# The weighed one-hot tile of the gate matrices: from a compare on VectorE and a multiply on ScalarE to one VectorE instruction per token

## The chip, the cores and the metric

The program runs on one core of one Trainium2 chip. The metric is the device time of one execution in microseconds (us). TensorE (PE) multiplies matrices into PSUM, VectorE (DVE), ScalarE (ACT) and GpSimd (POOL) work element by element on 128 partitions, and SyncE (SP) issues transfers. Each engine has a queue of its own and goes through it in order; engines wait for each other by semaphores.

## What is computed

One layer of a hybrid trunk for 576 frames (512 of a prompt, 64 of a running stream) of width 2048: two token mixers, then a retrieval of experts (PEER), then a norm. The change lies in the retrieval. Each token has 8 heads, each head picks 16 of 128 x 128 experts, and an expert's number is a pair of keys:

```python
idx = jnp.take_along_axis(cand_i, pos, axis=-1)          # i1 * 128 + i2
gate = jax.nn.softmax(best_s, axis=-1).astype(x.dtype)
...
hid = jax.nn.gelu(jnp.einsum('td,thkd->thk', xb, u_tab[ib]), approximate=False)
return jnp.einsum('thk,thkd->td', hid * gb, v_tab[ib])
```

For the first 384 tokens the kernel does not gather experts. It computes the hidden values of all 16384 experts and multiplies them by a gate matrix per token: 128 x 128 numbers, zero but for the up to 128 picks of the token. The other 192 tokens gather rows of the two tables.

## The kernel before

The matrix of one token is a product of two one-hot tiles over its 128 picks (8 heads x 16). Picks lie on the partitions. `i1T`, `i2T` and `gateT` (`idxT[0]` to `idxT[2]`, [128, 384]) hold, per pick and token, the first key, the second key and the gate. For a token, row p of the tile `oa` is zero but at key i1 of pick p, where the gate stands; row p of `ob` has a one at key i2. `ob` transposed times `oa` is the matrix.

Work goes in **units** of four tokens, 96 of them, in one stage of the program that is here called the gate stage:

- VectorE (`onehots`) compares the row `iota` (0 to 127) with four columns of `i1T` into `oa[u]` (128 x 512, four buffers, `NOH`), then the same for `i2T` into `ob[u]` (two buffers). Both are one TENSOR_TENSOR each, at L1669. An `oa` waits until TensorE has used that buffer four units ago, an `ob` until two units ago (`gmat_ps`).
- ScalarE (`weigh`, L1062) waits for `matched`, and multiplies each token's 128 x 128 part of `oa` in place by its column of `gateT`: four instructions per unit, one unit ahead. Then it copies the unit before out of PSUM (`gbuf`, L1074). After 12 units it also computes one GELU (L1081).
- TensorE (`gmats`, L2190) waits for `onehots` and `weighed`, and multiplies the unit's four tokens, 128 x 128 each, into one of four banks of `aux`.

TensorE has other work among these units: a **piece** is a weight block of 8 row blocks of 128, and each of its 8 steps is three matmuls of 128 x 384 (L1869). Six units stand in each piece, after steps 0, 2, 3, 5, 6 and 7 (`AFTER`), so the stage is 16 pieces. GpSimd prepares each piece once the one two before it is used: `wh` is a rounded copy of `wr` (L720), `wl` the rest (L722). SyncE loads the pieces, writes `gbuf` to memory after each 12 units and brings it back later as `gtile`. Before the gate stage VectorE picks the experts (top-k); behind it lie the value products with the streamed tables. All orders are written out by hand; there is no scheduler.

Of the kernel before, what the change touches and what calls it, by code (L numbers as in the profile page):

```python
# [17 lines left out]
ALU = mybir.AluOpType  # L18
ACT = mybir.ActivationFunctionType
# [6 lines left out]
TD = 384  # L26
# [12 lines left out]
NK = 128  # L39
# [4 lines left out]
TB = 48  # L44
NTB = TD // TB
# [14 lines left out]
NOH = 4  # L60
# [87 lines left out]
def trunk_program(nc, x_in, w_in, vec_in, const_in, s0_in, keys_in, u_in, v_in, y_out, sp_out, ss_out, dnc_out, scc_out,  # L148
# [49 lines left out]
    def const(name, rows=128):  # L198
        a, n = CONST[name]
        return cst[0:rows, a:a + n]  # L200

    def vector(name, j=None, n=1):
# [74 lines left out]
    oa = [r.take(f"oa{i}", [128, 4, NK]) for i in range(NOH)]  # L277
    ob = [r.take(f"ob{i}", [128, 4, NK]) for i in range(2)]
    gl = [sb(f"gl{i}", [128, TD], F32, gl_at + i * PC4) for i in range(2)]
    r = Region(rows_at, end)  # L280
    idxT = [r.take(n, [128, TD]) for n in ("i1T", "i2T", "gateT")]
# [56 lines left out]
        half_kept0 half_kept1 merged hb_in0 hb_in1 kept_z0 kept_z1 go_in0 go_in1 go_sq go_sum go_ss go_root go_step  # L338
        sig_kept0 sig_kept1 go_scaled go_hi go_lo
        mg_hi mg_lo xr_in0 xr_in1 keys_in score_ps topk_step scores_read shifted picked gate_exp pick_done pickT_ps  # L340
        pickT_done matched weighed onehots gmat_ps gmat_out gates_kept0 gates_kept1
        gt_in0 gt_in1 hid_kept0 hid_kept1 gl_in0 gl_in1 m_done m_hi m_lo tails_kept y_kept waited gelu_done alone_ready staged turned row_in0 row_in1 row_in2 row_in3 row_done raw_full2 hid_done coef_step sums_added""".split()
    S = {n: nc.alloc_semaphore(n) for n in names}

# [7 lines left out]
    def bank(slot, half):  # L352

        return ps[slot][:, half, 0:TD]
# [33 lines left out]
    def loop(eng, start, stop):  # L388

        return nc.Fori(start, stop, engines=bass.OrderedEngineSet([eng.engine]), hint_back_edge=True)  # L390

    def peel(eng, n, body):

        body(0)
        with loop(eng, 1, n) as i:
            body(i)
# [20 lines left out]
    UNITS = TB // 4  # L417
# [358 lines left out]
    def _(act):  # L776
# [76 lines left out]
        for g in range(2):  # L853
# [3 lines left out]
            last = act.activation(bar[:, 5:NCH, g, :],  # L857
                                  ps[0][:, 1, 5 * C - HT:HT].rearrange("p (n c) -> p n c", c=C), ACT.Copy)
# [24 lines left out]
        for v in range(H):  # L883
            m, u = 2 * H + v, v % 2
# [13 lines left out]
        for m in range(FIRST_Z, NZ):  # L898
            u = m % 2
# [155 lines left out]
                j += 1  # L1055

        def weigh(n, t0, u):

            act.wait_ge(S["matched"], n + 1)  # L1060
            for c in range(4):
                last = act.activation(oa[u][:, c, :], oa[u][:, c, :], ACT.Copy, scale=idxT[2][:, bass.ds(t0 + c, 1)])  # L1062
            last.then_inc(S["weighed"], 1)

        def gmats(i, final=False):
            for b in range(2):
                if not (isinstance(i, int) and i == 0):
                    act.wait_ge(S[f"gates_kept{b}"], 16 * i)
                for r_ in range(UNITS):
                    un = UNITS * b + r_  # L1070
                    if not (final and un == 2 * UNITS - 1):
                        weigh(2 * UNITS * i + un + 1, 2 * TB * i + 4 * un + 4, (un + 1) % NOH)
                    act.wait_ge(S["gmat_ps"], 2 * UNITS * i + un + 1)
                    act.activation(gbuf[b][:, :, 4 * r_:4 * r_ + 4],  # L1074
                                   aux[:, un % 4, :].rearrange("p (t i) -> p i t", t=4),
                                   ACT.Copy).then_inc(S["gmat_out"], 1)
                    hp = HPG + PLAIN + 2 * i + b
                    if r_ == UNITS - 1:
                        act.wait_ge(S[f"hid_kept{b}"], 16 * i + 16 * PLAIN // 2)
                        act.wait_ge(S["piece_used"], 2 * hp + 2)  # L1080
                        act.activation(gl[b][:, :], bank(b, 0), ACT.Gelu).then_inc(S[f"evacuated{b}"], 1)  # L1081

        weigh(0, 0, 0)
        gmats(0)
        with loop(act, 1, NTB // 2 - 1) as i:
            gmats(i)
        gmats(NTB // 2 - 1, True)

        def high(n, source):  # L1090
# [65 lines left out]
    def _(dve):  # L1156
        def wait(name, value):
            dve.wait_ge(S[name], value)
# [175 lines left out]
        for v in range(H):  # L1334
            u = v % 2
# [209 lines left out]
        for m in range(KD):  # L1545
            u = m % 2
# [117 lines left out]

        wait("pickT_done", 1)

        def alike(out, x, t0):

            return dve.tensor_tensor(out[:, :, :], const("iota").unsqueeze(1).to_broadcast([128, 4, NK]),  # L1669
                                     idxT[x][:, bass.ds(t0, 4)].unsqueeze(2).to_broadcast([128, 4, NK]),  # L1670
                                     ALU.is_equal)

        def onehots(i):
            for u in range(NOH):
                n = NOH * i + u
                if not isinstance(i, int):
                    wait("gmat_ps", n - NOH + 1)
                alike(oa[u], 0, 4 * n).then_inc(S["matched"], 1)
                if not (isinstance(i, int) and u < 2):
                    wait("gmat_ps", n - 1)  # L1680
                alike(ob[u % 2], 1, 4 * n).then_inc(S["onehots"], 1)

        peel(dve, TD // (4 * NOH), onehots)
        for u in range(2):
            wait(f"gates_kept{u}", 16 * NTB // 2)
# [10 lines left out]
        def kept_low(g, k):  # L1696

            n = G2 * g + k
            wait("m_hi", n + 1)
            dve.tensor_tensor(yp[:, n % (2 * G2), TD:2 * TD], gl[k % 2][:, :],  # L1700
                              yp[:, n % (2 * G2), 0:TD].bitcast(F32), ALU.subtract).then_inc(S["m_lo"], 1)
# [33 lines left out]
        def x_wide(b_):  # L1735

            if b_ == 0:
                dve.tensor_tensor(x_last[:, :, :], xa[:, :, TA - C:TA].bitcast(F32),
                                  xa[:, :, 2 * TA - C:2 * TA].bitcast(F32), ALU.add).then_inc(S["alone_ready"], 1)
                dve.tensor_tensor(held[:, :].rearrange("p (k t) -> p k t", t=128), xa[:, :, 0:128].bitcast(F32),  # L1740
                                  xa[:, :, TA:TA + 128].bitcast(F32), ALU.add).then_inc(S["staged"], 1)
            else:
                wait("alone_ready", 7)
                wait("turned", 2)
                dve.tensor_copy(held[:, :].rearrange("p (k c t) -> p k c t", c=2, t=C),
                                x_last[:, :, :].unsqueeze(2).to_broadcast([128, KD, 2, C])
                                ).then_inc(S["staged"], 1)
# [50 lines left out]
        kept_low(0, 0)  # L1798
        kept_gated(0, 1)
        kept_low(0, 1)  # L1800
        wait("weighed", TD // 4)
        x_wide(0)
        kept_gated(0, 2)
        kept_low(0, 2)
# [28 lines left out]
    def _(pe):  # L1833
# [27 lines left out]
        def piece(hp, c, slot, passes, k0, first, last, tiles_=range(NPIECE), done=("piece_used",),  # L1861
                  between=lambda t: None, ready=None):

            w = split_of(2 * hp + c) if isinstance(hp, int) and isinstance(c, int) else c % 2
            for t in tiles_:
                if ready:
                    ready(k0 + t)
                for weights, half, moving, more, final in passes(k0 + t - tiles_[0]):
                    mm_ = pe.matmul(ps[slot][:, half, 0:moving.shape[1]], weights[w][:, t, :], moving,  # L1869
                                    start=first and t == tiles_[0] and not more,  # L1870
                                    stop=last and t == tiles_[-1] and bool(final))
                if t < tiles_[-1]:
                    between(t)
            if done:
                mm_.then_inc(S[done[0]], 1)
# [302 lines left out]
        def gmats(i):  # L2178
            for b in range(2):
                hp = HPG + PLAIN + 2 * i + b  # L2180

                def unit(r_):
                    un = UNITS * b + r_
                    u = un % 4
                    pe.wait_ge(S["onehots"], 2 * UNITS * i + un + 1)
                    pe.wait_ge(S["weighed"], 2 * UNITS * i + un + 1)
                    if not (isinstance(i, int) and un < 4):
                        pe.wait_ge(S["gmat_out"], 2 * UNITS * i + un - 3)
                    for c in range(4):
                        last = pe.matmul(aux[:, u, c * NK:(c + 1) * NK], oa[un % NOH][:, c, :], ob[un % 2][:, c, :],  # L2190
                                         start=True, stop=True)
                    last.then_inc(S["gmat_ps"], 1)

                pe.wait_ge(S[f"evacuated{b}"], EV_G[b] + PLAIN // 2 + i)
                for c in range(2):
                    pe.wait_ge(S["lo_done"], 2 * hp + c + 1)
                    piece(hp, c, b, dense(xp, TD), NPIECE * c, c == 0, c == 1,
                          between=lambda t: unit(PER_PIECE * c + AFTER.index(t)) if t in AFTER else None)
                    unit(PER_PIECE * c + PER_PIECE - 1)
# [186 lines left out]
```

## Time and profile before

| | us |
|---|---|
| median of 3 runs | 4428.61 (4421.59 to 4431.16) |
| profiled execution, its own time | 4437.7 |
| its span in the trace | 4435.9 |
| PE busy | 4280.7 (97%) |
| DVE busy | 2552.9 (58%) |
| ACT busy | 1100.8 (25%) |
| POOL busy | 2657.0 (60%) |
| gate stage, first to last unit on TensorE | 2238.4 to 2422.5 |

The span is the time from the first to the last instruction in the trace. Busy shares are means over stages with different limits, so they don't say what the gate stage waits for. A duration in the trace reaches from an instruction's start to its end; successive instructions of one engine can overlap by a little, so from one start to the next it can be less than a duration.

### The profile page before, as it was taken

To read this page: it belongs to the slowest core of one execution; us is meant where nothing else is said; L and a number is where in the kernel's file an instruction comes from. 1 tells how busy PE (TensorE), PEld (TensorE's weight loads), DVE (VectorE), ACT (ScalarE), POOL (GpSimd) and SP (SyncE) were. 2 spreads that over 40 slices of the span, in tenths; PEclk is the share of its full clock that TensorE was granted. 3 is DMA by queue.
4 is the path that set the end of the run, shared out by engine and by line. 5 is a ranking of instruction groups with operands and counts; after the bars stand their busy time and mean duration, and the time that the engine had idled before them with its cause. 6 is when DMAs were issued, how large, how long until landed. Compare 5 with 4: busy or idle time off the path is not lost.

```text
span 4435.9 us, 73784 instructions
## 1 busy us (share of the span) xinstructions
PE 4280.7 (97%) x29840; PEld 4208.9 (95%) x29840; DVE 2552.9 (58%) x3551; ACT 1100.8 (25%) x1850; POOL 2657.0 (60%) x1516
## 2 busy tenths in 40 slices
PE   6999999999999999899999888999999999999997
PEld 6999999999999999899888888999999999999997
DVE  6863433322234421699577577777777776677744
ACT  4541000011011100100077122332322332323323
POOL 3555444444445555455743656888787787787863
PEclk9999999999999999999999999999999999999998
DMA  3333222222333443222446677999999998999963
GB/s 112 98 104 107 74 77 76 88 93 88 100 122 120 142 137 102 77 91 86 129 159 201 226 279 286 394 386 387 368 390 389 389 385 332 387 385 367 391 250 119
DMA packets 271697, 941.53 MB, mean 212 GB/s; under 512 B 59984, under 2 KB 101200, under 8 KB 221264
## 3 DMA queue, kind: packets, MB, share of 16 engines
q1 hardware_dynamic: 216144, 535.08, 35.1%
q0 software_dynamic: 55296, 402.68, 22.7%
q8 instruction: 203, 3.33, 0.3%
q14 instruction: 54, 0.44, 0.0%
HBM read 879.12 MB, written 58.55 MB: 211 GB/s over the span
## 4 chain that ended last, share of the span: by engine, by line
PE 80%; DVE 10%; DMA 4%; issue 2%; POOL 2%; ACT 1%; DVEq 0%; SPq 0%; ACTq 0%; POOLq 0%
PE ps L1869 74%; DMA wr<-in_w 3%; PE aux L2024 3%; POOL wl L771 2%; PE aux L2190 1%; DVE ob L1669 1%; DMA gl<-hid_s 1%; PE ps L1901 1%; DVE ti L1591 0%; DVE mrall L1592 0%; DVE ti L1599 0%; DVE cand L1601 0%; DVE sel L1630 0%; ACT wh L1112 0%; DVE sel L1635 0%
## 5 line engine op out<-in xcount | busy, mean ns | idle before, releaser
L771 POOL TENSOR_TENSOR wl<-wr,wh 128x1024 fp32r<-128x1024 f32 x444 | 1066.9, 2403 | 422.8 <-ACT wh L1112 421.5
L1869 PE MATMUL ps<-xp,wh 128*128 128x384 f32 x4544 | 1173.9, 339 | 9.8 <-POOL wl L722 6.8
L1869 PE MATMUL ps<-yp,wh 128*128 128x384 f32 x4096 | 1061.9, 340 | 37.0 <-POOL wl L771 15.0
L720 POOL CAST wh<-wr 128x1024 fp32r<-128x1024 f32 x338 | 369.0, 1092 | 1214.5 <-PE ps L1869 666.5
L1869 PE MATMUL ps<-xh,wh 128*128 128x288 f32 x3296 | 991.4, 301 | 1.6 <-DVE yt L1489 1.6
L1869 PE MATMUL ps<-xl,wh 128*128 128x288 f32 x3296 | 972.5, 295 | 0.0
L1869 PE MATMUL ps<-xh,wl 128*128 128x288 f32 x3296 | 969.1, 294 | 0.0
L722 POOL TENSOR_TENSOR wl<-wr,wh 128x1024 fp32r<-128x1024 f32 x338 | 839.6, 2484 | 27.1
L1869 PEld LDWEIGHTS ps<-xp,wh 128*128 128x128 f32 x4544 | 805.2, 189 | 12.1 <-issue 10.3
L1869 PEld LDWEIGHTS ps<-yp,wh 128*128 128x128 f32 x4096 | 750.7, 190 | 42.1 <-POOL wl L771 17.2
L1869 PE MATMUL ps<-xp,wl 128*128 128x384 f32 x2272 | 762.8, 336 | 0.0
L1112 ACT ACTIVATE wh<-wr 128x1024 fp32r<-128x1024 f32 x444 | 470.5, 1060 | 1043.4 <-PE ps L1869 680.0
L1869 PE MATMUL ps<-yp,wl 128*128 128x384 f32 x2048 | 696.0, 340 | 0.0
L1869 PEld LDWEIGHTS ps<-xh,wh 128*128 128x128 f32 x3296 | 617.6, 187 | 14.4 <-issue 5.4
L1869 PEld LDWEIGHTS ps<-xh,wl 128*128 128x128 f32 x3296 | 620.6, 188 | 0.0
L1869 PEld LDWEIGHTS ps<-xl,wh 128*128 128x128 f32 x3296 | 619.0, 188 | 1.0
L1766 DVE SCALAR_TENSOR_TENSOR aux<-rows,hid,aux 128x2048 f32<-128x2048 f32 x192 | 451.0, 2349 | 0.4
L1755 DVE SCALAR_TENSOR_TENSOR rows<-rows,aux 128x2048 f32<-128x2048 f32 x192 | 436.8, 2279 | 0.7 <-PE aux L2222 0.7
L1869 PEld LDWEIGHTS ps<-xp,wl 128*128 128x128 f32 x2272 | 428.3, 189 | 0.0
L1722 DVE TENSOR_TENSOR mg<-mg,ps 128x384 f32<-128x384 f32 x512 | 280.8, 551 | 253.1 <-PE ps L1869 252.8
L1869 PEld LDWEIGHTS ps<-yp,wl 128*128 128x128 f32 x2048 | 387.8, 189 | 0.0
L1709 DVE TENSOR_TENSOR ps<-ps,gtile 128x384 f32<-128x384 f32 x96 | 54.4, 567 | 322.0 <-ACT ps L1141 322.0
(295 smaller groups left out, 4382.6 us busy)
## 6 DMA issues: line engine op xcount, KB each, us to landing
wr<-in_w SPq DMA_DIRECT2D x786, 512.0 KB, 4.3
gates_s<-gbuf SPq DMA_DIRECT2D x8, 3072.0 KB, 11.8
gtile<-gates_s SPq DMA_DIRECT2D x32, 768.0 KB, 10.5
qkv<-qkv_s SPq DMA_DIRECT2D x9, 768.0 KB, 4.5
gl<-hid_s SPq DMA_DIRECT2D x32, 192.0 KB, 6.6
hid_s<-gl SPq DMA_DIRECT2D x28, 192.0 KB, 3.9
mg<-in_x SPq DMA_DIRECT2D x4, 1152.0 KB, 12.4
qkv_s<-lo SPq DMA_DIRECT2D x16, 288.0 KB, 3.0
```

What stands on the lines that cost most here:

```text
L720: pool.tensor_copy(high[u][:, :, :], wr[u][:, :, :]).then_inc(S["hi_done"], 1)
L722: pool.tensor_tensor(low[u][:, :, :], wr[u][:, :, :], high[u][:, :, :].bitcast(F32), ALU.subtract).then_inc(S["lo_done"], 1)
L771: pool.tensor_tensor(wl[q][:, :, :], wr[r_][:, :, :], wh[q][:, :, :].bitcast(F32), ALU.subtract).then_inc(S["lo_done"], 1)
L1112: act.activation(wh[q][:, :, :], wr[r_][:, :, :], ACT.Copy).then_inc(S["hi_done"], 1)
L1669: return dve.tensor_tensor(out[:, :, :], const("iota").unsqueeze(1).to_broadcast([128, 4, NK]), idxT[x][:, bass.ds(t0, 4)].unsqueeze(2).to ...
L1709: dve.tensor_tensor(own, own, gtile[g % 2][:, :, k, :], ALU.mult).then_inc(S["m_done"], 1)
L1722: dve.tensor_tensor(mg[:, j, 0:TD], mg[:, j, 0:TD], bank(x, d % 2), ALU.add).then_inc(S[f"evacuated{x}"], 1)
L1755: dve.scalar_tensor_tensor(rows[r_][:, :], rows[r_][:, :], 1.0, wide_aux, ALU.mult, ALU.mult, accum_out=hid[b_][:, j:j + 1]).then_inc(S["r ...
L1766: dve.scalar_tensor_tensor(wide_aux, rows[r_][:, :], hid[b_][:, j:j + 1], wide_aux, ALU.mult, ALU.add).then_inc(S["row_done"], 1)
L1869: mm_ = pe.matmul(ps[slot][:, half, 0:moving.shape[1]], weights[w][:, t, :], moving, start=first and t == tiles_[0] and not more, stop=las ...
L1901: mm_ = pe.matmul(ps[x][:, half, 0:moving.shape[1]], held[:, t, :], moving, start=k == 0 and not more, stop=k == KD - 1 and bool(final))
L2024: last = pe.matmul(out(h), left(h), right(h), start=start, stop=stop)
```

## The change

VectorE writes the weighed `oa` itself: per token one TENSOR_SCALAR that compares `iota` with the token's column of `i1T` and multiplies the result by its column of `gateT`, both given as one value per partition. ScalarE's `weigh` and the semaphores `matched` and `weighed` are gone. The order of the two tiles on VectorE, the buffers and the other waits stay.

```diff
@@ -1055,21 +1055,12 @@
                 j += 1
 
 
-        def weigh(n, t0, u):
-
-            act.wait_ge(S["matched"], n + 1)
-            for c in range(4):
-                last = act.activation(oa[u][:, c, :], oa[u][:, c, :], ACT.Copy, scale=idxT[2][:, bass.ds(t0 + c, 1)])
-            last.then_inc(S["weighed"], 1)
-
-        def gmats(i, final=False):
+        def gmats(i):
             for b in range(2):
                 if not (isinstance(i, int) and i == 0):
                     act.wait_ge(S[f"gates_kept{b}"], 16 * i)
                 for r_ in range(UNITS):
                     un = UNITS * b + r_
-                    if not (final and un == 2 * UNITS - 1):
-                        weigh(2 * UNITS * i + un + 1, 2 * TB * i + 4 * un + 4, (un + 1) % NOH)
                     act.wait_ge(S["gmat_ps"], 2 * UNITS * i + un + 1)
                     act.activation(gbuf[b][:, :, 4 * r_:4 * r_ + 4],
                                    aux[:, un % 4, :].rearrange("p (t i) -> p i t", t=4),
@@ -1080,11 +1071,7 @@
                         act.wait_ge(S["piece_used"], 2 * hp + 2)
                         act.activation(gl[b][:, :], bank(b, 0), ACT.Gelu).then_inc(S[f"evacuated{b}"], 1)
 
-        weigh(0, 0, 0)
-        gmats(0)
-        with loop(act, 1, NTB // 2 - 1) as i:
-            gmats(i)
-        gmats(NTB // 2 - 1, True)
+        peel(act, NTB // 2, gmats)
 
 
         def high(n, source):
@@ -1664,21 +1651,28 @@
 
         wait("pickT_done", 1)
 
-        def alike(out, x, t0):
+        def chosen(out, t0):
 
             return dve.tensor_tensor(out[:, :, :], const("iota").unsqueeze(1).to_broadcast([128, 4, NK]),
-                                     idxT[x][:, bass.ds(t0, 4)].unsqueeze(2).to_broadcast([128, 4, NK]),
+                                     idxT[1][:, bass.ds(t0, 4)].unsqueeze(2).to_broadcast([128, 4, NK]),
                                      ALU.is_equal)
+
+        def chosen_weighed(out, t0):
+
+            for c in range(4):
+                last = dve.tensor_scalar(out[:, c, :], const("iota"), idxT[0][:, bass.ds(t0 + c, 1)],
+                                         idxT[2][:, bass.ds(t0 + c, 1)], ALU.is_equal, ALU.mult)
+            return last
 
         def onehots(i):
             for u in range(NOH):
                 n = NOH * i + u
                 if not isinstance(i, int):
                     wait("gmat_ps", n - NOH + 1)
-                alike(oa[u], 0, 4 * n).then_inc(S["matched"], 1)
+                chosen_weighed(oa[u], 4 * n)
                 if not (isinstance(i, int) and u < 2):
                     wait("gmat_ps", n - 1)
-                alike(ob[u % 2], 1, 4 * n).then_inc(S["onehots"], 1)
+                chosen(ob[u % 2], 4 * n).then_inc(S["onehots"], 1)
 
         peel(dve, TD // (4 * NOH), onehots)
         for u in range(2):
@@ -1798,7 +1792,7 @@
         kept_low(0, 0)
         kept_gated(0, 1)
         kept_low(0, 1)
-        wait("weighed", TD // 4)
+        wait("gmat_ps", TD // 4)
         x_wide(0)
         kept_gated(0, 2)
         kept_low(0, 2)
@@ -2183,7 +2177,6 @@
                     un = UNITS * b + r_
                     u = un % 4
                     pe.wait_ge(S["onehots"], 2 * UNITS * i + un + 1)
-                    pe.wait_ge(S["weighed"], 2 * UNITS * i + un + 1)
                     if not (isinstance(i, int) and un < 4):
                         pe.wait_ge(S["gmat_out"], 2 * UNITS * i + un - 3)
                     for c in range(4):
```

```order
L1669 ISA [waits gmat_ps]
L1669 TENSOR_TENSOR oa_147<-cst,i1T 128x512
L1158 REGISTER_ALU
L1669 REGISTER_ALU [waits gmat_ps]
L1669 TENSOR_TENSOR ob_151<-cst,i2T 128x512
```

The same place in the changed kernel:

```order
L1663 ISA [waits gmat_ps]
L1663 TENSOR_SCALAR oa_147<-cst,i1T,gateT 128x128
L1663 ISA
L1663 TENSOR_SCALAR oa_147<-cst,i1T,gateT 128x128
L1663 ISA
L1663 TENSOR_SCALAR oa_147<-cst,i1T,gateT 128x128
L1663 ISA
L1663 TENSOR_SCALAR oa_147<-cst,i1T,gateT 128x128
L1145 REGISTER_ALU
L1656 REGISTER_ALU [waits gmat_ps]
L1656 TENSOR_TENSOR ob_151<-cst,i2T 128x512
```

One instruction of 512 columns with two tensors has become four of 128 columns with one tensor and two values per partition, each with an ISA row ahead; `ob` is as it was, and so are both waits.

ScalarE, in the body of its loop, one unit of the kernel before:

```order
L1062 ISA [waits matched]
L1062 ACTIVATE oa_149<-oa_149,gateT 128x128
L1062 ISA
L1062 ACTIVATE oa_149<-oa_149,gateT 128x128
L1062 ISA
L1062 ACTIVATE oa_149<-oa_149,gateT 128x128
L1062 ISA
L1062 ACTIVATE oa_149<-oa_149,gateT 128x128
L1074 ACTIVATE gbuf_145<-aux 128x128x4 [waits gmat_ps]
L1060 REGISTER_ALU
```

Three units of the changed kernel, at the same place:

```order
L1065 ACTIVATE gbuf_145<-aux 128x128x4 [waits gmat_ps]
L1064 REGISTER_ALU
L1065 ACTIVATE gbuf_145<-aux 128x128x4 [waits gmat_ps]
L1064 REGISTER_ALU
L1065 ACTIVATE gbuf_145<-aux 128x128x4 [waits gmat_ps]
L1064 REGISTER_ALU
```

The four multiplies and the wait for VectorE are gone from ScalarE; only the copy out of PSUM stands in a unit.

## Rows read from the trace of the kernel before

**Rows 1.** The page's chain that ended last, share of the span by line.

```profile
PE ps L1869 74%; DMA wr<-in_w 3%; PE aux L2024 3%; POOL wl L771 2%; PE aux L2190 1%; DVE ob L1669 1%; DMA gl<-hid_s 1%; PE ps L1901 1%; DVE ti L1591 0%; DVE mrall L1592 0%; DVE ti L1599 0%; DVE cand L1601 0%; DVE sel L1630 0%; ACT wh L1112 0%; DVE sel L1635 0%
```

**Rows 2.** Stretch, length, busy us (count) of PE, PEld, DVE, ACT, POOL; clock; DMA share, GB/s.

```profile
2240.00:2290.00 50.00, 45.48 (x315) 40.88 (x314) 45.16 (x53) 44.29 (x133) 15.17 (x9) 1.00 0.41 132
2440.00:2450.00 10.00, 6.29 (x27) 6.32 (x28) 3.80 (x4) 1.05 (x2) 6.86 (x5) 0.83 0.77 266
```

**Rows 3.** Groups of instructions in the stage, 2238 to 2424 us.

```profile
L1062 ACT ACTIVATE oa<-oa,gateT 128x128 f32<-128x128 f32 x382 | 121.4, 393 | 21.2 <-DVE oa L1669 21.2
L2190 PE MATMUL aux<-ob,oa 128*128 128x128 f32 x768 | 106.4, 281 | 18.6 <-DVE ob L1669 11.7 <-issue 3.9 <-ACT oa L1062 2.6
L1669 DVE TENSOR_TENSOR ob<-cst,i2T 128x512 f32<-128x512 f32 x94 | 97.8, 1040 | 85.3 <-PE aux L2190 83.4
...
L1074 ACT ACTIVATE gbuf<-aux 128x512 f32<-128x512 f32 x96 | 56.0, 583 | 1.3 <-PE aux L2190 1.0
...
L720 POOL CAST wh<-wr 128x1024 fp32r<-128x1024 f32 x16 | 16.6, 1037 | 124.3 <-issue 62.4 <-PE ps L1869 61.9
```

**Rows 4.** Instructions in order of time: the first unit, and one piece.

```profile
2238.44 1.13 PE L2190 MATMUL aux<-ob,oa 128*128 128x128 f32 x8 [1.37 <-ACT oa L1062]
...
2251.42 1.16 PE L2190 MATMUL aux<-ob,oa 128*128 128x128 f32 x8 [0.81 <-DVE ob L1669]
...
2252.00 1.28 ACT L1062 ACTIVATE oa<-oa,gateT 128x128 f32<-128x128 f32 x4 [1.56 <-DVE oa L1669]
...
2253.38 1.13 PE L2190 MATMUL aux<-ob,oa 128*128 128x128 f32 x8 [0.28 <-issue]
...
2255.42 1.05 PE L2190 MATMUL aux<-ob,oa 128*128 128x128 f32 x8
...
2256.84 1.06 PE L2190 MATMUL aux<-ob,oa 128*128 128x128 f32 x8
...
2258.58 1.04 POOL L720 CAST wh<-wr 128x1024 fp32r<-128x1024 f32 x1 [7.77 <-issue]
2258.63 1.53 DVE L1669 TENSOR_TENSOR oa<-cst,i1T 128x512 f32<-128x512 f32 x1
...
2259.70 2.71 POOL L722 TENSOR_TENSOR wl<-wr,wh 128x1024 fp32r<-128x1024 f32 x1
...
2260.09 2.87 DVE L1669 TENSOR_TENSOR ob<-cst,i2T 128x512 f32<-128x512 f32 x1
...
2262.88 0.68 DVE L1669 TENSOR_TENSOR oa<-cst,i1T 128x512 f32<-128x512 f32 x1
...
2263.01 1.16 PE L2190 MATMUL aux<-ob,oa 128*128 128x128 f32 x8 [0.79 <-DVE ob L1669]
...
2263.48 0.68 DVE L1669 TENSOR_TENSOR ob<-cst,i2T 128x512 f32<-128x512 f32 x1
```

**Rows 5.** Lines and tiles: duration ns min/median/max, first and last start us, forms.

```profile
L1669 DVE TENSOR_TENSOR oa<-cst,i1T x96: 677/684/1551, 2169.1 to 2418.5; 128x512 f32<-128x512 f32 x96
...
L1165 DVE TENSOR_SCALAR gr<-gr x8: 459/460/461, 1310.3 to 1468.7; 128x576 f32<-128x576 f32 x8
...
L1474 DVE TENSOR_SCALAR scv<-scb,vec x8: 508/509/2735, 438.9 to 781.1; 128x578 f32<-128x578 f32 x8
...
L1622 DVE TENSOR_SCALAR posi<-posu x8: 189/190/196, 1870.8 to 2148.0; 128x80 uint32<-128x80 uint32 x8
...
L1189 DVE SCALAR_TENSOR_TENSOR mg<-mg,vec,ms x16: 814/814/819, 4419.5 to 4430.4; 128x576 f32<-128x576 f32 x16
...
L2190 PE MATMUL aux<-ob,oa x768: 270/275/377, 2238.4 to 2422.5; 128*128 128x128 f32 x192
```

**Rows 6.** Groups and timeline of VectorE in the last stretch, from 4412 us.

```profile
L1181 DVE SCALAR_TENSOR_TENSOR ms<-ms,rst 128x576 f32<-128x576 f32 x1 | 0.8, 757 | 0.0
...
4419.51 11.76 DVE L1189 SCALAR_TENSOR_TENSOR mg<-mg,vec,ms 128x576 f32<-128x576 f32 x16
```

More of the change, by code:

```diff
@@ L340, in trunk_program @@
         mg_hi mg_lo xr_in0 xr_in1 keys_in score_ps topk_step scores_read shifted picked gate_exp pick_done pickT_ps
-        pickT_done matched weighed onehots gmat_ps gmat_out gates_kept0 gates_kept1
+        pickT_done onehots gmat_ps gmat_out gates_kept0 gates_kept1
         gt_in0 gt_in1 hid_kept0 hid_kept1 gl_in0 gl_in1 m_done m_hi m_lo tails_kept y_kept waited gelu_done alone_ready staged turned row_in0 row_in1 row_in2 row_in3 row_done raw_full2 hid_done coef_step sums_added""".split()
```

## The prediction

> **What bounds the kernel now.** I read the page's chain first, to see which engine sets the end. TensorE's matmuls at L1869 hold 74% of the span, and the lines of the change (L2190, L1669) hold 1% each [rows 1]. So the change can only be worth what its own stage is worth, and I go to that stage.
>
> The stretch view shows it as the place where three engines are almost full at once: in 50 us PE is busy for 45.5, VectorE for 45.2, ScalarE for 44.3 [rows 2]. Busy time alone doesn't say who waits. The groups do: TensorE stood idle ahead of the unit matmuls for 18.6 us, 11.7 of it until VectorE's `ob` was done and 2.6 until ScalarE's multiply was. ScalarE stood idle for 21.2 us until VectorE's `oa` was there. VectorE's 83.4 us of idle time until PE is mostly one long wait ahead of the stage [rows 3].
>
> The timeline of one piece says where this comes from. Unit matmuls start at 2251.42, 2253.38, 2255.42, 2256.84 and, one piece after the first, at 2263.01: a piece takes 11.59 us [rows 4]. With nothing late, two units with one step of matmuls between them are 1.42 us apart (2255.42 to 2256.84). A piece is 6 units and 8 steps. With two steps between them they are 2.04 apart (2253.38 to 2255.42), which may hold a short wait. So TensorE's own work is at most 4 x 1.42 + 2 x 2.04 = 9.8 us per piece, and 1.8 us or more of each piece are waits.
>
> The largest wait is at GpSimd's pair of instructions. POOL starts its copy at 2258.58, VectorE its `oa` at 2258.63. That `oa` takes 1.53 us where the median is 0.68, the `ob` behind it 2.87, and the next `oa` starts at 2262.88 [rows 4, 5]. From 2262.88 to 2263.48 one step of VectorE's queue takes 0.60 us. So two steps worth 1.20 took 4.25, and the pair costs VectorE 3.05 us. GpSimd is held up in its turn: VectorE's instruction runs between the copy and the subtraction. I read it as one of the two standing still while the other runs. The fast TENSOR_SCALAR of L1474 is met by this too: its median is 0.51, its longest 2.74 [rows 5].
>
> Behind this stall ScalarE adds a second, smaller one: `oa` is done, then the four multiplies start at 2252.00 and take 1.28 us, and TensorE's second unit starts at 2253.38, 1.96 after the first, not 1.42 [rows 4].
>
> **What the change removes.** 384 ScalarE instructions (382 of them in the window, 121.4 us busy [rows 3]). None of this time is on the path in itself. What goes is the 0.54 us behind each stall, and, at the start, 1.37 us: the first unit waited that long for ScalarE, which had a GELU to do first [rows 4]. VectorE begins its first `oa` at 2169.1, long before [rows 5].
>
> ScalarE keeps 0.58 us per unit [rows 3] and is far from any bound. PE's and ScalarE's removed semaphore waits cost nothing of their own.
>
> **What it adds.** VectorE's 96 compares of 512 columns become 384 TENSOR_SCALAR of 128. No row has this instruction with two values per partition, so I build it from neighbours.
>
> - Without such values: 460 ns at 576 columns, 190 at 80 [rows 5], so 0.544 ns per column, and 216 ns at 128 columns. The distance between starts is shorter than the duration: 0.68 against 0.60 for L1669, so 0.08 less [rows 4, 5]. That makes 0.136 us per instruction.
> - One value per partition: 509 ns at 578 columns against 460 + 1, so 48 ns [rows 5]. For SCALAR_TENSOR_TENSOR it is 814 against 757, so 57; and sixteen of them in a row take 11.76 us, (11.76 - 0.81) / 15 = 0.730 from start to start, against 0.757 - 0.08 = 0.677, so 53 [rows 5, 6]. The price is therefore paid in the distance too, not hidden by overlap.
> - Two values: no row. From below they cost nothing between starts (0.136 us per instruction, a rival), or no more than one does (0.184); from above each costs up to 57 (0.250). I take two full prices and 0.245, since the first one is paid in full.
> - The other open price is the mode. 757 against 460 ns at 576 columns [rows 5, 6] is 0.516 ns per column that an SBUF-to-SBUF TENSOR_SCALAR saves. If compare-and-multiply doesn't get that, each costs 66 ns more, 0.31 us. L1165 also has two operations (a multiply and an add), and L1474 has the value per partition, and both are fast, so I don't expect it.
>
> A unit then takes VectorE 4 x 0.245 + 0.60 = 1.58 us, where it was 1.20. This is where the gain goes. VectorE was the engine that stalled TensorE, with slack to catch up between stalls; now it has none.
>
> **The sum.** Per piece VectorE needs 6 x 1.58 + 3.05 = 12.53 us. TensorE needs at most 9.8. So VectorE sets the pace, and a piece goes from 11.59 to 12.53. The first piece's GpSimd pair falls ahead of the stage and the last one's behind it: 15 stalls lie inside. 15 x 0.94 = 14.1, less 1.4 at the start: **+12.7 us**.
>
> A second way bounds this. 96 units x 1.58 = 151.7, plus 15 x 3.05 = 45.8, less what is made ahead (three `oa`, two `ob`: 4.1 us), is 193.4, and it begins when the first unit's matmuls (1.1 us) are done: about 194.7 from first to last unit. Now it is 2238.4 to about 2421.6 (its last matmul starts at 2422.5, 0.9 into the unit) [rows 5], 183.2. That gives +11.5 - 1.4 = +10.1. It credits the whole lead, which the two `ob` buffers will partly waste. I take +12.
>
> Nothing gives it back: behind the stage everything hangs on it, since the gate matrices must be written to memory before VectorE can go on, and TensorE has but a few products to cover that. In 2440 to 2450, PE is busy for 6.3 of 10 us already [rows 2]. GpSimd waits for TensorE between its pairs for 7.8 us [rows 4] and bears shorter interruptions. The transfers have room at a share of 0.41 [rows 2].
>
> On its own time, the profiled execution goes from 4437.7 to 4450; it lies 9 us above the median of the runs. On the median: 4428.6 + 12 = **4441**.
>
> **The rivals.**
>
> - *The second value is fetched with the first* (0.184 to 0.193 us). 6 x (4 x 0.188 + 0.60) + 3.05 = 11.2 per piece: 15 x -0.4 - 1.4 = -7, **4421**. For it: nothing in the trace; against it: the first one is paid in full. Chance 0.16.
> - *The values cost nothing between starts* (0.136). VectorE would need 6 x (0.544 + 0.60) + 3.05 = 9.9 per piece, and TensorE would nearly be the bound. But it would still stand still behind GpSimd's pair, for the 0.8 us of now, since two `ob` buffers cover no more. Of the 1.8 us of waits 1.0 would go: 16 x -1.0 - 1.4 = -17, **4411**. This is the side where the change is faster by more than the noise, and it decides from 0.186 us per instruction downward. Against it: 0.730 from start to start. Chance 0.08.
> - *The instruction costs 0.31 us*, by the slow mode, by dearer fetches or by its sequencer rows. 6 x (1.24 + 0.60) + 3.05 = 14.1 per piece, 15 x 2.5 - 1.4 = +36, **4465**. Half way, at 0.28, it is +25. If the slow mode also let VectorE run on beside GpSimd, some of the 3.05 us would come back; `ob` with its two tensors would still stand still. Chance 0.15.
> - *TensorE's clock falls.* Now its gaps are 0.8 us; each would grow to 1.58 + 3.05 less the work between two units, 2.6 or more. In 2240 to 2290 full clock (2.4 GHz) was granted, in 2440 to 2450, with gaps, 0.83 of it, a mix with 1.2 GHz [rows 2]. Matmuls at half clock take twice as long, but there are 2.7 us of room per piece. It decides only where over 2.7 us of a piece's matmuls run slowly. Chance 0.04, with +30.
> - *The stage is longer, and the end isn't*, because a transfer behind it was late anyway. I see no such wait long enough. Chance 0.07, 4429.
>
> The Trainium skill (VectorE: DVE Perf Modes, "The TRN2 errata") has 58 cycles plus the columns over the mode's factor for an SBUF-to-SBUF instruction, at 0.96 GHz: an estimate of 127 ns here, which would be the second rival: by that price alone the sum would be its -17. The same section warns that many small tiles pay the fixed part per tile and wants 512 columns or more; this change goes the other way. The rows of L1189 stand against the 58 cycles, and I go by them.
>
> **How the numbers follow.** The forecast has a chance of 0.50; its own range, for 0.232 to 0.256 us and a few us of noise between medians, is 4434 to 4449. What a measurement of this kernel can tell from no change is about 0.2%, 9 us. Faster: the second rival and some of the first, 0.14. Same: the rest of the first, the last, and the low end of the forecast (a price under 0.236), 0.27. Slower: 0.59. The range leaves out the second rival and the far half of the third: 4418 to 4458.
>
> **What the changed profile would show.** TENSOR_SCALAR `oa` at about 0.32 us median, its starts 0.245 apart; a piece 12.5 us long; VectorE busy all through the stage with little idle time until PE; TensorE's idle time ahead of L2190 all put to VectorE, some 3 us per piece; ScalarE busy for a third of before; POOL's subtraction at 2.4 to 2.6, not 2.71. The forecast is wrong if the starts lie under 0.21 apart, or if pairs of GpSimd cost VectorE clearly other than 3.05 us now that its instructions are short.

## The result, and the profile after

The changed kernel takes 4447.0 us (median of 6 runs, 4442.2 to 4454.8), the kernel before, timed beside it, 4428.3 (4421.6 to 4432.1). The ratio is 1.0044, with a 95% interval of 1.0032 to 1.0057: 19 us slower, of which the interval allows 14 to 25. The forecast was 12 us slower.

The page of the changed kernel: busy us and instructions of each engine, and the chain by line.

```profile
PE 4278.9 (96%) x29840; PEld 4215.7 (95%) x29840; DVE 2591.2 (58%) x3839; ACT 997.7 (22%) x1466; POOL 2656.6 (60%) x1516
...
PE ps L1863 75%; DMA wr<-in_w 3%; PE aux L2018 3%; PE aux L2183 2%; POOL wl L771 1%; PE ps L1895 1%; DVE oa L1663 1%; DVE ti L1578 0%; DVE mrall L1579 0%; DVE ob L1656 0%; DVE ti L1586 0%; DVE cand L1588 0%; DVE sel L1617 0%; DVE sel L1622 0%; DVE sel L1597 0%
```

VectorE has 288 instructions more (3839), ScalarE 384 fewer and 103 us less of work; the chain is TensorE's as before [rows 1]. The groups in the gate stage, busy time, mean duration, idle time ahead and who ended it:

```profile
L1663 DVE TENSOR_SCALAR oa<-cst,i1T,gateT 128x128 f32<-128x128 f32 x372 | 145.4, 449 | 1.1 <-issue 1.1
L2183 PE MATMUL aux<-ob,oa 128*128 128x128 f32 x760 | 107.2, 286 | 36.4 <-DVE ob L1656 36.3
...
L1656 DVE TENSOR_TENSOR ob<-cst,i2T 128x512 f32<-128x512 f32 x94 | 65.6, 698 | 63.4 <-PE aux L2183 63.3
L1065 ACT ACTIVATE gbuf<-aux 128x512 f32<-128x512 f32 x96 | 57.4, 598 | 143.9 <-PE aux L2183 143.9
```

TensorE's idle time ahead of the unit matmuls has doubled, from 18.6 us to 36.4, and all of it now ends with VectorE's `ob`; there is none left until ScalarE [rows 3]. ScalarE has little to do and waits 143.9 us for TensorE. VectorE's 63.3 us until PE are the one wait ahead of the stage (61.0) and four short ones in it (2.3). From the first unit to the last matmul it was 2238.4 to 2422.5, a length of 184.1 [rows 5]. Now it is 2236.4 to 2439.4, 203.0.

The new instruction (duration min/median/max), its sequencer rows, the unit matmuls, and the first unit that VectorE makes, ahead of the stage and with fixed addresses:

```profile
L1663 DVE TENSOR_SCALAR oa<-cst,i1T,gateT x384: 328/334/2552, 2169.1 to 2437.5; 128x128 f32<-128x128 f32 x192
L1663 DVEq FUSED_REGOPS  x368: 69/69/94, 2239.7 to 2435.4; - x184
...
L2183 PE MATMUL aux<-ob,oa x768: 270/275/465, 2236.4 to 2439.4; 128*128 128x128 f32 x192
...
2169.08 1.12 DVE L1663 TENSOR_SCALAR oa<-cst,i1T,gateT 128x128 f32<-128x128 f32 x4 [2.59 <-ACT gateT L1042]
2170.11 0.68 DVE L1656 TENSOR_TENSOR ob<-cst,i2T 128x512 f32<-128x512 f32 x1
```

0.334 us is the median, and four of them take 2170.11 - 2169.08 = 1.03 us from start to start, 0.257 each. The prediction had 0.32 and 0.245. Here no address is computed, and yet the distance is that of the loop (2314.84 - 2313.82 = 1.02 us for four, below), so the sequencer rows cost nothing.

One piece in order of time:

```profile
2309.30 3.99 DVE L1663 TENSOR_SCALAR oa<-cst,i1T,gateT 128x128 f32<-128x128 f32 x4
...
2309.76 1.04 POOL L720 CAST wh<-wr 128x1024 fp32r<-128x1024 f32 x1 [8.35 <-issue]
...
2310.87 2.34 POOL L722 TENSOR_TENSOR wl<-wr,wh 128x1024 fp32r<-128x1024 f32 x1
...
2313.22 0.68 DVE L1656 TENSOR_TENSOR ob<-cst,i2T 128x512 f32<-128x512 f32 x1
...
2313.82 1.10 DVE L1663 TENSOR_SCALAR oa<-cst,i1T,gateT 128x128 f32<-128x128 f32 x4
...
2313.95 1.16 PE L2183 MATMUL aux<-ob,oa 128*128 128x128 f32 x8 [2.83 <-DVE ob L1656]
...
2314.84 0.68 DVE L1656 TENSOR_TENSOR ob<-cst,i2T 128x512 f32<-128x512 f32 x1
```

Undisturbed, a unit takes VectorE 2314.84 - 2313.22 = 1.62 us. At GpSimd's pair the four `oa` take 2313.22 - 2309.30 = 3.92 us, not 1.03: 2.89 lost, close to the 3.05 of the kernel before [rows 4]. Behind it TensorE has stood still for 2.83 us, where it was 0.79. GpSimd's first and last copy that bear on the stage:

```profile
2245.25 1.04 POOL L720 CAST wh<-wr 128x1024 fp32r<-128x1024 f32 x1 [5.82 <-PE ps L1863]
...
2438.80 1.04 POOL L720 CAST wh<-wr 128x1024 fp32r<-128x1024 f32 x1 [8.08 <-issue]
```

These are 15 pieces in 193.55 us, 12.90 each. The same two of the kernel before start at 2246.99 and 2421.86: 174.87 us, 11.66 each. So the stage lost 18.7 us over 15 pieces, and gained 2.0 at its start (2238.4 to 2236.4). Of these 1.37 were the wait for ScalarE [rows 4]; by the rest the start moves from one trace to the next anyway (2234.4 to 2237.8 in the kernels made from the changed one).

### The profile page after: what moved, and what is told of

Same layout as the page of the kernel before. It is cut to its first block, busy times and chain, and to the rows that moved or that the text cites. A ratio compares the mean times of both kernels' runs of the same rounds, so it can differ in the third digit from the quotient of the medians.

```text
span 4445.9 us, 73784 instructions
## 1 busy us (share of the span) xinstructions
PE 4278.9 (96%) x29840; PEld 4215.7 (95%) x29840; DVE 2591.2 (58%) x3839; ACT 997.7 (22%) x1466; POOL 2656.6 (60%) x1516
## 4 chain that ended last, share of the span: by engine, by line
PE 82%; DVE 9%; DMA 3%; issue 2%; POOL 2%; ACT 1%; DVEq 0%; SPq 0%; ACTq 0%; POOLq 0%
PE ps L1863 75%; DMA wr<-in_w 3%; PE aux L2018 3%; PE aux L2183 2%; POOL wl L771 1%; PE ps L1895 1%; DVE oa L1663 1%; DVE ti L1578 0%; DVE mrall L1579 0%; DVE ob L1656 0%; DVE ti L1586 0%; DVE cand L1588 0%; DVE sel L1617 0%; DVE sel L1622 0%; DVE sel L1597 0%
```

## The experiments

Each kernel was timed beside the kernel before; the times below are medians, with the ratio to the kernel before in that comparison. "A piece" is the time from GpSimd's first copy that bears on the stage to its last, 15 pieces later, over 15. Where ScalarE makes the copies, GpSimd's subtractions are taken.

**One value per partition.** The compare alone:

```diff
-                last = dve.tensor_scalar(out[:, c, :], const("iota"), idxT[0][:, bass.ds(t0 + c, 1)],
-                                         idxT[2][:, bass.ds(t0 + c, 1)], ALU.is_equal, ALU.mult)
+                last = dve.tensor_scalar(out[:, c, :], const("iota"), idxT[0][:, bass.ds(t0 + c, 1)],
+                                         None, ALU.is_equal)
```

> The changed kernel with the compare alone: TENSOR_SCALAR takes i1T, and the multiply by gateT is left out (one value per partition, so the gates are missing from the result). Theory A, each value per partition is fetched at its full price: starts 0.20 us apart (0.257 less 0.057), a unit of 0.80 + 0.60 = 1.40, a piece of 8.4 + 3.1 = 11.5 us, so 4447 - 15 x 1.4 = 4426, no slower than the kernel before. Theory B, the time lies in the instruction's fixed part, its two operations or its sequencer rows, and not in the second value: starts stay at 0.24 or more, 4441 or more.

4425.0 against 4426.1, ratio 0.9996 (0.9987 to 1.0005); a piece takes 11.33 us. One unit on VectorE, its `oa` and the start of its `ob`:

```profile
2262.87 0.87 DVE L1663 TENSOR_SCALAR oa<-cst,i1T 128x128 f32<-128x128 f32 x4
2263.65 0.69 DVE L1656 TENSOR_TENSOR ob<-cst,i2T 128x512 f32<-128x512 f32 x1
```

0.78 us for four, 0.195 each. 0.062 us less per instruction, 384 times, and with it the whole loss of the change is gone. Theory B falls as far as it was the fixed part or the sequencer rows. But the multiply went together with its value; whether the second operation has a price of its own is settled by the next run.

**No value per partition.**

```diff
-                last = dve.tensor_scalar(out[:, c, :], const("iota"), idxT[0][:, bass.ds(t0 + c, 1)],
-                                         idxT[2][:, bass.ds(t0 + c, 1)], ALU.is_equal, ALU.mult)
+                last = dve.tensor_scalar(out[:, c, :], const("iota"), 3.0, 1.0, ALU.is_equal, ALU.mult)
```

> The changed kernel with two constants (3.0 and 1.0) for the two values per partition: indices and gates of oa are left out, everything else stays. Theory A: starts 0.14 us apart, VectorE needs 6 x 1.16 + 3.1 = 10.1 us per piece, TensorE at most 9.8 and the part of GpSimd's pair that two ob buffers don't cover (0.8 us): pieces of 10.3 to 10.9, 4447 - 15 x 2.3 = about 4412. Theory B (the fixed part of four small instructions is what costs, whatever they read): starts at 0.20 or more, 4426 or more.

4416.1, ratio 0.9982 (0.9973 to 0.9992); a piece takes 11.03 us.

```profile
2263.60 0.69 DVE L1656 TENSOR_TENSOR ob<-cst,i2T 128x512 f32<-128x512 f32 x1 [0.70 <-PE aux L2182]
...
2269.80 0.62 DVE L1663 TENSOR_SCALAR oa<-cst 128x128 f32<-128x128 f32 x4
2270.34 0.68 DVE L1656 TENSOR_TENSOR ob<-cst,i2T 128x512 f32<-128x512 f32 x1
```

2270.34 - 2269.80 = 0.54 for four, 0.135 each. This kernel has both operations and neither value, so the operations cost nothing here, and none, one and two values give 0.135, 0.195 and 0.257. But the piece is longer than expected, and the time 4 us above: VectorE now waits for TensorE (0.70 us at 2263.60) because both `ob` are in use, and cannot build the lead that would carry it over the next pair of GpSimd. VectorE's own work fills these 11.03 us at a price of about 0.19 us: (11.03 - 2.89) / 6 = 1.36 per unit, less 0.60 for `ob`, over four. Below that the two buffers should set the time; this is an estimate, no run has a price between 0.135 and 0.195.

**GpSimd's pair at a quarter of its length**, in the gate stage of the changed kernel:

```diff
-            pool.tensor_copy(high[u][:, :, :], wr[u][:, :, :]).then_inc(S["hi_done"], 1)
+            pool.tensor_copy(high[u][:, 0:n, :], wr[u][:, 0:n, :]).then_inc(S["hi_done"], 1)
...
-        on(P_F // 2 + 3, HPV)
+        on(P_F // 2 + 3, HPG + PLAIN + 1)
+        on(HPG + PLAIN + 1, HPG + PLAIN + 9, 2)
+        on(HPG + PLAIN + 9, HPV)
```

(and the subtraction likewise)

> The changed kernel with GpSimd's pair at a quarter of its columns in the gate stage (three quarters of wh and wl are left unprepared there, so 16 pieces of hidden values are wrong). Theory A, VectorE stands still while GpSimd runs and is throughput-bound: the pair costs it 0.6 us, not 3.1, a piece is 9.8 + 0.6 = 10.4 us, 4447 - 15 x 2.5 = 4410. Rival: GpSimd's pair only coincides with the stall, and VectorE is slow for itself; then a piece stays at 12.9 and the time at 4447.

4405.3, ratio 0.9963 (0.9949 to 0.9976); a piece takes 10.42 us. The groups in the stage:

```profile
L2185 PE MATMUL aux<-ob,oa 128*128 128x128 f32 x740 | 101.6, 280 | 5.8 <-DVE ob L1658 5.6 <-ACT gbuf L1067 0.2
...
L722 POOL TENSOR_TENSOR wl<-wr,wh 128x256 fp32r<-128x256 f32 x16 | 16.9, 1057 | 1.3
```

TensorE's wait for `ob` falls to 5.6 us. A piece is 2.5 us shorter than in the changed kernel, of 3.1 at stake. The rival is out: it is GpSimd's pair that stops VectorE.

**The same in the kernel before.** The edit above, applied to it.

> The kernel before with GpSimd's pair at a quarter of its columns in the gate stage (three quarters of wh and wl are left unprepared there, so 16 pieces of hidden values are wrong). It pairs with the short pair in the changed kernel (4405, 10.3 us per piece). Theory A, the change costs only because VectorE's 1.63 us per unit and GpSimd's 3.1 us per piece add up: without the pair ScalarE's 1.65 us per unit and TensorE set the pace, about 10.3 us per piece, 4429 - 15 x 1.3 = 4408, so that the changed kernel is level with it. Rival: the four small instructions cost TensorE time of their own; then the kernel before gains as much here as the changed one did (42 us) and reaches 4390.

4402.5, ratio 0.9945 (0.9929 to 0.9961); a piece takes 10.16 us. The kernel before gains 25 us here; the changed one, 19 us behind it at full length, ends beside it (4402.5 and 4405.3, and the intervals of the two ratios overlap). By the pieces 15 x (10.42 - 10.16) = 4 us are left of 19. So the dearer unit costs as much as it does only because GpSimd's pair has already taken VectorE's spare time.

**The change undone, with a third `ob` buffer.**

```diff
+    ob.append(r.take("ob2", [128, 4, NK]))
...
-            for u in range(NOH):
-                n = NOH * i + u
-                if not isinstance(i, int):
+            for u in range(3 * NOH):
+                n = 3 * NOH * i + u
+                if not (isinstance(i, int) and u < NOH):
                     wait("gmat_ps", n - NOH + 1)
-                alike(oa[u], 0, 4 * n).then_inc(S["matched"], 1)
-                if not (isinstance(i, int) and u < 2):
-                    wait("gmat_ps", n - 1)
-                alike(ob[u % 2], 1, 4 * n).then_inc(S["onehots"], 1)
+                alike(oa[u % NOH], 0, 4 * n).then_inc(S["matched"], 1)
+                if not (isinstance(i, int) and u < 3):
+                    wait("gmat_ps", n - 2)
+                alike(ob[u % 3], 1, 4 * n).then_inc(S["onehots"], 1)
```

(and `ob[un % 3]` on TensorE)

> The kernel before, the change undone, with a third ob buffer (VectorE may be three units ahead, not two). Theory A: in the kernel before VectorE had spare time (7.2 + 3.05 = 10.3 of 11.6 us per piece) and only the lead was too short for GpSimd's pair; a third buffer lets it work ahead, ScalarE at 1.65 us per unit is next, a piece takes 10.4 to 10.7 us, 4428 - 15 x 1.1 = 4412. Rival: VectorE is at its limit in the kernel before too; then the third buffer changes nothing, 4428.

4404.6, ratio 0.9962 (0.9948 to 0.9975); a piece takes 10.31 us. The groups in the stage, and a pair of GpSimd in order of time:

```profile
L1063 ACT ACTIVATE oa<-oa,gateT 128x128 f32<-128x128 f32 x379 | 120.8, 396 | 1.9 <-DVE oa L1670 1.4
L2191 PE MATMUL aux<-ob,oa 128*128 128x128 f32 x768 | 105.1, 280 | 3.0 <-ACT oa L1063 1.4 <-DVE ob L1670 1.2 <-issue 0.2
...
2258.08 2.70 POOL L723 TENSOR_TENSOR wl<-wr,wh 128x1024 fp32r<-128x1024 f32 x1
...
2258.47 2.86 DVE L1670 TENSOR_TENSOR oa<-cst,i1T 128x512 f32<-128x512 f32 x1
...
2259.66 1.12 PE L2191 MATMUL aux<-ob,oa 128*128 128x128 f32 x8
...
2261.25 0.68 DVE L1670 TENSOR_TENSOR ob<-cst,i2T 128x512 f32<-128x512 f32 x1
...
2261.31 1.13 PE L2191 MATMUL aux<-ob,oa 128*128 128x128 f32 x8
```

The stop is still there: the `oa` at 2258.47 takes 2.86 us, as long as the `ob` that was hit in the kernel before (2.87 [rows 4]). But one unit starts on TensorE in its course, at 2259.66, and the next at 2261.31, 0.06 us after VectorE has begun the next `ob`; that unit's own `ob` was made before the stop. TensorE's idle time ahead of the units is 3.0 us in the whole stage, not 18.6. ScalarE works without a gap now (1.9 us of idle time ahead of its multiplies, where it had 21.2) and sets the pace at 1.65 us per unit. The gain is larger than expected (4412), as the piece is shorter than the 10.4 to 10.7 us of theory A.

**A third `ob` buffer in the changed kernel**, the same edit.

> The changed kernel with a third ob buffer, the same edit that gave the kernel before 22 us. Theory A, VectorE is throughput-bound in the changed kernel (6 x 1.63 + 3.1 = 12.9 us per piece against 9.8 on TensorE): a lead cannot be built, nothing or a few tenths per piece come back (what falling clock and uneven pieces cost), 4440 to 4447. Rival: the lead is what lacks here as well, and the buffer takes some 20 us, 4427.

4443.8, ratio 1.0033 (1.0021 to 1.0045); a piece takes 12.66 us. What is worth 22 us in the kernel before brings 0.24 us per piece here, 15 x 0.24 = 4 us, and the interval overlaps that of the changed kernel, so by the times alone the gain isn't shown. A buffer carries an engine over a stop only if it has spare time to fill it.

**ScalarE makes `wh`**, in the changed kernel, for 16 pieces; GpSimd keeps the subtraction:

```diff
+                    if r_ % PER_PIECE == 0:
+                        c = r_ // PER_PIECE
+                        x, q = HPG + PLAIN + 2 * i + b + c, 1 - c
...
+                        act.wait_ge(S[f"raw_full{q}"], 16 * x + 16)
+                        act.wait_ge(S["piece_used"], 2 * x + q - 1)
...
+                        act.activation(wh[q][:, :, :], wr[q][:, :, :], ACT.Copy).then_inc(S["hi_done"], 1)
```

> The changed kernel, and ScalarE, idle for two thirds of the stage now, makes the rounded copy wh of 16 pieces in GpSimd's place; GpSimd keeps the subtraction. Theory A: the pair of 3.1 us becomes a single stop of about 2.2, a piece 9.8 + 2.2 = 12.0, 4447 - 15 x 0.9 = 4433, still slower than before. Rival: GpSimd's copy does not hold VectorE up and only the subtraction does: no change, 4447.

4429.9 against 4429.2, ratio 1.0003 (0.9992 to 1.0014); a piece takes 11.82 us.

```profile
2283.76 1.06 ACT L1085 ACTIVATE wh<-wr 128x1024 fp32r<-128x1024 f32 x1
2284.19 0.71 DVE L1678 TENSOR_TENSOR ob<-cst,i2T 128x512 f32<-128x512 f32 x1
...
2284.79 3.19 DVE L1685 TENSOR_SCALAR oa<-cst,i1T,gateT 128x128 f32<-128x128 f32 x4
2284.90 2.49 POOL L765 TENSOR_TENSOR wl<-wr,wh 128x1024 fp32r<-128x1024 f32 x1 [9.59 <-ACT wh L1085]
...
2287.90 0.68 DVE L1678 TENSOR_TENSOR ob<-cst,i2T 128x512 f32<-128x512 f32 x1
```

ScalarE's copy at 2283.76 doesn't touch VectorE, whose `ob` starts 0.43 us later and takes its usual 0.7. The subtraction at 2284.90 does: four `oa` take 2287.90 - 2284.79 = 3.11 us, 2.1 lost and not 2.9. So both of GpSimd's instructions hold VectorE up, and the rival is out. With this the changed kernel is level with the one before. Its freed ScalarE is worth something here because it takes work from GpSimd that stops VectorE.

**One token in four on VectorE, and `wh` on ScalarE**, from the kernel before:

```diff
-                alike(oa[u], 0, 4 * n).then_inc(S["matched"], 1)
+                part(oa[u], 4 * n).then_inc(S["matched"], 1)
+                chosen_weighed(oa[u], 4 * n)
```

(`part` compares three tokens, `chosen_weighed` the fourth, `weigh` multiplies three)

> The kernel before, with one of a unit's four tokens weighed by VectorE's compare-and-multiply and three by ScalarE, and ScalarE making wh as well. Theory A: VectorE 0.47 + 0.26 + 0.60 = 1.33 per unit, 8.0 + 2.2 = 10.2 us per piece; ScalarE 6 x 1.37 + 1.1 + 0.2 = 9.5; TensorE 9.8 at most, and what two ob buffers leave uncovered: 10.4 to 10.8 us per piece, 4427 - 15 x 1.0 - 1 = 4411. Rival: ScalarE's copy, 1.06 us long in one go, delays its multiplies so that TensorE waits for them: 11.3 or more, 4422 or more.

4411.6, ratio 0.9964 (0.9951 to 0.9977); a piece takes 10.38 us, and 10.19 over the first 12. The waits in the stage, us in total and times:

```profile
PEld aux L2225 <- issue: 6.7, 9, 3.0
PEld aux L2225 <- DVE ob L1691: 6.6, 13, 0.8
ACT oa L1074 <- DVE oa L1703: 6.2, 13, 0.7
```

Neither ScalarE nor VectorE is waited for by much. The thirteenth piece is another matter, it takes 14.8 us:

```profile
2372.14 0.39 ACT L1074 ACTIVATE oa<-oa,gateT 128x128 f32<-128x128 f32 x1
...
2375.45 0.69 ACT L1074 ACTIVATE oa<-oa,gateT 128x128 f32<-128x128 f32 x2 [2.92 <-issue]
...
2376.25 1.13 PE L2225 MATMUL aux<-ob,oa 128*128 128x128 f32 x8 [2.73 <-issue]
```

In the midst of a unit's three multiplies ScalarE stood still for 2.9 us, for nothing that the profile shows, and TensorE with it. The cause stays open. It is there once in this trace and once, at the same place, in that of the next kernel (2.88 us, 14.8 us for the piece), and such a piece is 4.6 us longer than the ones before it.

**The same with a third `ob` buffer.**

> The same with a third ob buffer. Theory A: bound by VectorE's 10.2 us per piece or TensorE's 9.8, so 10.0 to 10.3, 4403, about as fast as the kernel before with a third buffer (4405, 10.31 us per piece, where ScalarE's 1.65 us per unit sets the pace). Rival: ScalarE's long copy costs as above, 4410 or more.

4406.8, ratio 0.9954 (0.9939 to 0.9969); a piece takes 10.42 us (10.25 over the first 12). It can't be told from the kernel before with the third buffer alone (4404.6, ratio 0.9962, 10.31 us per piece), which needs the smallest edit. Both lie within 0.6 us of TensorE's own work, 9.8 us at most.

## Why the prediction was right, and where it was off

- *The gate stage decides, and nothing else.* Right. ScalarE's 384 instructions went without any gain but the start: it is 2.0 us earlier, not 1.4, and the 0.6 between is no more than the start moves by itself.
- *VectorE becomes the pace maker, by 6 units plus GpSimd's pair.* Right. TensorE waits for it alone, though for 36.4 / 15 = 2.4 us per piece and not some 3. With the pair shortened 4 of 19 us are left, and the third buffer tells the two kernels apart: 22 us where VectorE has spare time, about 4 where it has none.
- *The price of the new instruction.* Right in its parts, low in its size. I took 0.245 us from between the bounds; it is 0.257, above the upper bound of 0.250. Each value per partition costs 0.06 us from start to start, where I had read 0.048 to 0.057. So the rival in which the second value comes free (0.184 to 0.193) is out, as is 0.31. The fast mode holds without values: 0.135 against the 0.136 that I had worked out. With two values it is less plain, because the second adds 0.062 us, and the slow mode would add 0.066, and no row has such an instruction at another width.

What speaks for the fast mode with two values as well is that GpSimd stops the instruction. In the same trace VectorE reduces `sel`, one tensor in SBUF, in 1482 ns for 1280 columns, 1.16 ns per column and so at the slow rate. GpSimd's pair runs at the same time, and neither waits for the other:

```profile
1921.13 1.04 POOL L720 CAST wh<-wr 128x1024 fp32r<-128x1024 f32 x1 [4.47 <-PE ps L1863]
1921.27 2.88 DVE L1627 TENSOR_REDUCE pick<-sel 128x1280 f32 x2 [0.22 <-DVE sel L1622]
1922.24 2.39 POOL L722 TENSOR_TENSOR wl<-wr,wh 128x1024 fp32r<-128x1024 f32 x1
...
L1627 DVE TENSOR_REDUCE pick<-sel x16: 1475/1482/1487, 1880.8 to 2161.9; 128x1280 f32 x16
```

- *The unit and the piece.* This is the term that was mis-sized: 1.63 us (1.03 + 0.60), not 1.58, times 6 is 0.3 us more per piece. The whole difference is 12.90 - 12.53 = 0.37; the 0.07 left are the two terms of the next point (0.23 - 0.16).
- *GpSimd's pair costs 3.05 us.* It costs 2.89, 0.16 less. So of the piece 12.90 - 9.78 - 2.89 = 0.23 us are something else, which the sum had put at nothing: VectorE waits for TensorE after all, where TensorE's clock has fallen. GpSimd's subtraction, which I expected at 2.4 to 2.6 us, takes 2.34 to 2.40 in 12 of the 16, and 2.83 to 3.09 in the other four.

Busy time and granted clock of three stretches of the changed kernel, then a unit after a stop, and VectorE's four waits for TensorE in the stage:

```profile
2240.00:2290.00 50.00, 40.16 (x277) 37.93 (x277) 48.33 (x115) 14.56 (x26) 14.60 (x8) 0.97 0.36 114
2310.00:2320.00 10.00, 7.17 (x54) 6.84 (x53) 10.00 (x23) 2.77 (x5) 3.13 (x2) 1.00 0.59 181
2340.00:2350.00 10.00, 10.00 (x68) 10.00 (x67) 9.34 (x29) 2.99 (x5) 0.47 (x1) 0.85 1.03 345
...
2339.37 1.97 PE L2183 MATMUL aux<-ob,oa 128*128 128x128 f32 x8 [2.92 <-DVE ob L1656]
...
2254.54 0.69 DVE L1656 TENSOR_TENSOR ob<-cst,i2T 128x512 f32<-128x512 f32 x1 [0.58 <-PE aux L2183]
2344.18 0.69 DVE L1656 TENSOR_TENSOR ob<-cst,i2T 128x512 f32<-128x512 f32 x1 [0.66 <-PE aux L2183]
2370.18 0.69 DVE L1656 TENSOR_TENSOR ob<-cst,i2T 128x512 f32<-128x512 f32 x1 [0.45 <-PE aux L2183]
2421.67 0.69 DVE L1656 TENSOR_TENSOR ob<-cst,i2T 128x512 f32<-128x512 f32 x1 [0.58 <-PE aux L2183]
```

The granted clock was 0.97 of full in the first stretch, 1.00 in the second and 0.85 in the third, where it is a mix of 2.4 and 1.2 GHz; in the kernel before it had been 1.00 in 2240 to 2290 [rows 2]. After a stop of 2.9 us a unit takes 1.97 us, not 1.16, and soon after VectorE waits 0.66 us for TensorE. It is the fourth rival, in small: I had said that the room in a piece covers it, and it mostly does. The four waits add up to 2.27 us, 0.15 per piece of the 0.23. They lie in four pieces of 14.4 to 14.6 us, and the stretch of 10 us around each has a granted clock of 0.83 to 0.93. The third `ob` buffer in the changed kernel bears this out: there two waits for TensorE of 0.2 us are left, although the clock falls to 0.66 in two stretches of 10 us, and a piece takes 12.66 us, where 6 x 1.63 + 2.89 is 12.67. The last 0.08 I can't assign.

- *The sum.* By the measured parts: 15 x (12.90 - 11.66) = 18.7, less 2.0 at the start, 16.7; the end of the stage moved from 2422.5 to 2439.4, 16.9. The medians moved by 18.8, and the interval of 14 to 25 holds both. I had taken 12 where my first way gave 12.7 and the second 10.1; the second credits VectorE's lead in full (and has a slip of 0.2: 193.4 and 1.1 are 194.5), and the first was short by the price of the instruction.
- *Nothing gives it back.* Right by the medians. The two profiled executions lie only 10 us apart in span, but the one of the kernel before lies 9 us above its median. Behind the stage its trace has 2013.4 us and that of the changed kernel 2006.5; over all eleven traces this part varies between 1992 and 2013 us, so single traces can't decide it.
- *The second rival* (values free) had the right kind of limit, what two `ob` buffers don't cover, but put it at 11.6 - 1.0 = 10.6 us per piece, where the kernel without values takes 11.03; and it had the wrong price.
- *The rule of the Trainium skill* (VectorE: DVE Perf Modes, "The TRN2 errata"), 58 cycles plus the columns over the mode's factor, gives an estimate of 127 ns. The kernel without values per partition has 135 from start to start and 212 to 220 as a duration. So the rule is near for the distance of instructions with constants, and misses 60 ns for every value per partition. Its warning about many small tiles agrees in part: of the 0.135 us only 0.070 go by columns (128 at 0.544 ns), so some 0.065, an estimate, is paid per instruction and four times a unit. But what made the change slower is the values, since without them it is faster than the kernel before (0.9982).

## What to carry to other kernels

Price a replaced instruction by the distance from start to start, with a term for each operand that it fetches per partition, and multiply by the count before believing that one instruction is cheaper than two on two engines. Before moving work off an engine, look at which one the bound engine waits for, and what holds *that* one up; here VectorE was nearly full (10.3 of 11.66 us per piece) and stopped by GpSimd, so shortening the stop was worth 25 us and a third buffer to work ahead 22, and giving it ScalarE's work cost 19. In these kernels a deeper buffer helped the engine that was stopped but had time to spare, and hardly the one that had none.

## What the runs showed of the hardware

- TENSOR_SCALAR of 128 x 128 fp32 from SBUF to SBUF: 0.135, 0.195 and 0.257 us from start to start with none, one and two values per partition (durations 0.22, 0.28 and 0.334).
- Compare-and-multiply with two constants runs in the fast mode (0.135 us); with two values per partition only the stops speak for it. VectorE stands still for GpSimd in it as it does with two tensors: 2.89 us lost per pair of 1.04 and 2.34 us. A TENSOR_REDUCE of one tensor at the slow rate is not stopped by such a pair (1475 to 1487 ns in all 16). ScalarE's copy of the same tile (1.06 us) doesn't stop it.
- Computed addresses cost nothing here: four instructions take 1.03 us in the part without a loop and 1.02 in the loop, where each instruction has a row of 0.069 us in the sequencer.
- TensorE's granted clock fell to 0.83 to 0.93 in some stretches of 10 us, in four of 15 pieces, after stops of 2.8 to 3.1 us; after another stop of 2.83 us (2310 to 2320) it stayed at 1.00. In the kernel before, with stops of 0.8 us, it was 1.00 throughout the stage.
